# End of slots, end of output projections and operand rings in a two-layer diffusion backbone on one core

## Reference, cut to what matters

```python
def even_mixer(h_lat, h_ctx, ...):        # layer 0
    z = h_lat @ w_in
    a = spatial_gating(z[..., :1024])     # 4 groups of 128, chunks of 128 positions
    q, k, v = ...                         # 8 heads, 2 key/value heads, 128 wide, rmsnorm, rotary
    return concatenate([a, attention(q, k, v)]) @ w_out          # 1536 -> 1024 (and the context's)

def odd_mixer(h_lat, h_ctx, ...):         # layer 1
    c = silu(layernorm(dwconv31(a * sigmoid(g))))                # 512 channels
    q = rmsnorm(z_q) @ w_uq; k, v = rmsnorm(z_kv) @ w_ukv        # 8 heads, 128 + 64 rotary
    return concatenate([c, attention(q, k, v)]) @ w_out          # 1536 -> 1024

def conv_ffn(h, w_in, conv_w, conv_b, w_out):
    z = h @ w_in                                                 # 1024 -> 2 x 2816
    return (silu(dwconv3(z[..., :2816])) * z[..., 2816:]) @ w_out

# every layer
x = x + gate1 * rmsnorm(mixer(rmsnorm(x, g1) * (1 + scale1) + shift1))
x = x + gate2 * rmsnorm(conv_ffn(rmsnorm(x, g3) * (1 + scale2) + shift2))
```

## Time and profile before

| | |
|---|---|
| median of 3 runs | 1823.19 us (1819.68 to 1828.9) |
| profiled execution, its time | 1824.78 us |
| profiled execution, its span | 1823.0 us |
| TensorE busy | 1750.0 us, 96% |
| VectorE, ScalarE, GpSimd busy | 1121.0, 684.2, 182.0 us |
| mean granted clock of TensorE | 0.988 |
| HBM read | 163.31 MB, 91 GB/s |

### The profile page before, as it was taken

One profiled execution on the slowest core, in us unless ns is written; L12 is line 12 of the kernel. 1 busy time (PEld: TensorE's weight loads), 2 busy tenths in 40 slices (PEclk: granted clock), 3 DMA queues, 4 the chain that ended last, 5 costly groups with the idle time before them and its releaser, 6 DMA issues.

```text
span 1823.0 us, 23635 instructions
## 1 busy us (share of the span) xinstructions
PE 1750.0 (96%) x9274; PEld 1470.9 (81%) x9274; DVE 1121.0 (61%) x1662; ACT 684.2 (38%) x1123; POOL 182.0 (10%) x200
## 2 busy tenths in 40 slices
PE   6999999999999999999999999999989899999998
PEld 4777899777888888887777888789977788887776
DVE  4776777777676765644444578778766544444554
ACT  4343256544422121223243444354545433223342
POOL 1077400001200000000000110111210200000000
PEclk9999999999999999999999999999999899999999
DMA  9433100131234335421112122200012132222221
GB/s 363 145 118 105 46 1 1 58 104 47 104 130 148 141 136 196 172 106 70 69 50 90 47 95 71 77 17 1 2 70 71 50 111 92 92 102 105 92 94 68
DMA packets 30994, 166.77 MB, mean 91 GB/s; under 512 B 4144, under 2 KB 4656, under 8 KB 16688
## 3 DMA queue, kind: packets, MB, share of 16 engines
q1 hardware_dynamic: 29024, 163.60, 24.6%
q10 hardware_dynamic: 1872, 1.82, 0.4%
HBM read 163.31 MB, written 2.10 MB: 91 GB/s over the span
## 4 chain that ended last, share of the span: by engine, by line
PE 85%; DVE 7%; ACT 3%; issue 2%; DVEq 1%; DMA 1%; POOL 0%; ACTq 0%; SPq 0%
PE PS L292 12%; PE PS L294 12%; PE PS L296 12%; PE PS L582 8%; PE PS L584 7%; PE PS L583 7%; PE PS L1085 5%; PE PS L319 3%; PE PS L320 3%; PE PS L321 3%; PE PS L1070 2%; DVE w_lo L281 2%; DVE cat_od L2040 1%; DVE pre_tmp_pre L486 1%; ACT w_hi L275 1%
## 5 line engine op out<-in xcount | busy, mean ns | idle before, releaser
L292 PE MATMUL PS<-HT,w_hi 128*128 128x512 f32 (+1 forms) x1232 | 378.3, 355 | 10.6 <-DVE HT L492 5.0
L294 PE MATMUL PS<-HT,w_hi 128*128 128x512 f32 (+1 forms) x1232 | 370.1, 349 | 0.0
L296 PE MATMUL PS<-HT,w_lo 128*128 128x512 f32 (+1 forms) x1232 | 370.0, 349 | 0.0
L281 DVE TENSOR_TENSOR w_lo<-w_raw,w_hi 128x2048 fp32r<-128x2048 f32 x103 | 237.8, 2309 | 154.1 <-ACT w_hi L275 149.6
L582 PE MATMUL PS<-w_hi,a_ring 128*128 128x512 f32 x680 | 274.9, 404 | 13.7 <-DVE a_ring L658 5.6
L583 PE MATMUL PS<-w_lo,a_ring 128*128 128x512 f32 x680 | 266.5, 392 | 0.0
L292 PEld LDWEIGHTS PS<-HT,w_hi 128*128 128x128 f32 x1232 | 206.5, 189 | 52.0 <-issue 7.0
L275 ACT ACTIVATE w_hi<-w_raw 128x2048 fp32r<-128x2048 f32 x103 | 196.4, 1907 | 135.9 <-PEq L616 69.3
L296 PEld LDWEIGHTS PS<-HT,w_lo 128*128 128x128 f32 x1232 | 206.7, 189 | 31.0
L294 PEld LDWEIGHTS PS<-HT,w_hi 128*128 128x128 f32 x1232 | 206.9, 189 | 30.8
L957 DVE SCALAR_TENSOR_TENSOR yb<-PS,cws,yb 128x511 f32<-128x511 f32 (+1 forms) x132 | 83.2, 658 | 168.9 <-ACTq L923 164.6
(11 more groups left out here) (305 smaller groups left out, 2596.5 us busy)
## 6 DMA issues: line engine op xcount, KB each, us to landing
w_raw<-wpack SPq DMA_DIRECT2D x103, 1024.0 KB, 4.8
m_raw<-modu SPq DMA_DIRECT2D x80, 512.0 KB, 4.0
mod_raw<-modw SPq DMA_DIRECT2D x8, 1024.0 KB, 12.0
X<-x SPq DMA_DIRECT2D x1, 2048.0 KB, 8.3
out<-X SPq DMA_DIRECT2D x4, 512.0 KB, 2.6
X<-ctx SPq DMA_DIRECT2D x1, 1024.0 KB, 10.6
alnb<-aln ACTq DMA_DIRECT2D x1, 512.0 KB, 4.2
csn<-rope_ev ACTq DMA_DIRECT2D x1, 256.0 KB, 2.6
```

The costliest lines, as they stand in the source:

```text
L281: nc.vector.tensor_tensor(w_lo[r][:, :], w_raw[r][:, :], w_hi[r][:, :].bitcast(F32), ALU.subtract).then_inc(wl_ready, 1)
L292: nc.tensor.matmul(o, wh, xh, start=start, stop=False)
L294: nc.tensor.matmul(o, wh, xl, start=False, stop=False)
L296: last = nc.tensor.matmul(o, wl, xh, start=False, stop=stop)
```

## The change

Four things are done together.

1. The drains at slot ends go. `w_used` of a slot is raised by the first matmul of the next slot, `a_used` of a column half's last part by the second matmul of the next half.
2. The ends of `evo`, `ffo0` and `odo` go by pairs of token tiles: both first quads of a pair, then both second quads; transposes of tiles 0 and 1 stand ahead of the second quads of the last pair. The orders of ScalarE, VectorE and GpSimd follow. `pre3` has eight transposes ahead too, and four of its eight affines are on ScalarE, with a drain each.
3. Parts are in rings of three; the feed-forward projections' first three parts are made ahead: 0 and 1 before the last slot is evacuated, 2 within it. In `ffo0` token tile 5 of q=0 and q=1 is made after q=1. Gate rows of the feed-forward projections start at q=3, the diagonal of the first at q=0.
4. odo's first weight turn is at q=3, not q=1. The channel norm starts at unit 22; the convolution has three steps a unit up to unit 13; the reciprocal is in two halves, in units 29 and 30; `beside_out` is spread over q=0, 2, 3, 4 (norm) and q=4, 6, 7 (SiLU).

The diff, cut to its core:

```diff
-        def split_mm(outs, wh, wl, xs, start, stop):
+        def split_mm(outs, wh, wl, xs, start, stop, slot_done=False, parts_done=None):
 
             last = None
-            for o, (xh, _) in zip(outs, xs):
-                nc.tensor.matmul(o, wh, xh, start=start, stop=False)
-            for o, (_, xl) in zip(outs, xs):
-                nc.tensor.matmul(o, wh, xl, start=False, stop=False)
+            for i, (o, (xh, _)) in enumerate(zip(outs, xs)):
+                mm = nc.tensor.matmul(o, wh, xh, start=start, stop=False)
+                if slot_done and i == 0:
+                    mm.then_inc(w_used, 1)
+            for i, (o, (_, xl)) in enumerate(zip(outs, xs)):
+                mm = nc.tensor.matmul(o, wh, xl, start=False, stop=False)
+                if parts_done is not None and i == 0:
+                    mm.then_inc(parts_done, 8)
...
+        def pre_affine_high(act, st, layer, which, i0, i1):
+
+            for i in range(i0, i1):
+                act.wait_ge(S(st, "tr"), since(st, "tr") + i + 1)
+                if i >= 6:
+                    low = "lo_odd" if i % 2 else "lo_even"
+                    act.wait_ge(S(st, low), since(st, low) + (i - 6) // 2 + 1)
+                nc.scalar.activation(pre_tmps[st][i % 6][:, :], PS[:, pre_bank(st, i), 0:256], ACT.Identity,
+                                     bias=modc[:, layer, 3 * which * KD + i, 0:1], scale=prescale[:, i, 0:1])\
+                    .then_inc(S(st, "aff"), 1)
+                act.drain()
+                nc.scalar.activation(HT[:, 0, 0, i, :], pre_tmps[st][i % 6][:, :], ACT.Copy).then_inc(S(st, "hi"), 1)
...
+                        first = g == 0 and mt == 0 and k == 0
                         last = split_mm([o], w_hi[r][:, cols], w_lo[r][:, cols], [(HT[:, g, 0, k, :], HT[:, g, 1, k, :])],
-                                        k == 0, k == KD - 1)
+                                        k == 0, k == KD - 1, first, S("evo", "a_used") if first else None)
...
-        def a_high(q, kt):
-
-            return a_ring[q % 2] if q < kt else a_ring[(q - kt) % 8]
+        def first_of_ffn(st, q):
+
+            return q == 0 and st in ("ffo0", "ffo1")
+
+        def second_of_ffn(st, q):
+
+            return q == 1 and st in ("ffo0", "ffo1")
+
+        def a_high(st, q, kt):
+
+            if q >= kt:
+                return a_ring[(q - kt + 6) % 8]
+            return a_ring[6] if first_of_ffn(st, q) else (a_second if second_of_ffn(st, q) else a_ring[q % 3])
+
+        def a_low(st, q):
+
+            return a_ring[7] if first_of_ffn(st, q) else a_ring[3 + q % 3]
...
-                    if q == 2 and before is not None:
+                c = q - (2 if before is None else 3)
+                if 0 <= c < len(gate_chunks(tiles)):
...
+                held = before is not None and tiles == NT and q < 2
+                for t in range(NT - 1 if held else tiles):
                     if h == 1 and k == 0:
...
-                    last = products(q, j, h, k, n, t)
+                    last = products(q, j, h, k, n, t, q > 0 and t == 0 and (j == 0 or k == 0), h == 1 and t == 0 and k == 0)
                     if k == kt - 1:
                         last.then_inc(S(st, "acc"), 1)
-                if k == kt - 1:
-                    pe.drain().then_inc(S(st, "a_used"), 1)
-                else:
+                if held and q == 1:
+                    pe.wait_ge(S(before, "evac"), JF)
+                    for p, (_, jp, hp, kp) in enumerate(out_ktiles(kt)[0:2]):
+                        products(p, jp, hp, kp, n, NT - 1).then_inc(S(st, "a_used"), 1)
+                elif k < kt - 1 and not held:
                     last.then_inc(S(st, "a_used"), 1)
-                if j == 3:
-                    pe.drain().then_inc(w_used, 1)
...
-            four(0, 0)
-            for t in range(1, tiles):
+            for t in range(0, tiles, 2):
                 four(0, t)
-                if chunk is not None and t == 1:
+                four(0, t + 1)
+                if chunk is not None and t == 0:
                     m_sum(pe, chunk)
-                if chunk is not None and t == 2:
-                    m_turn(pe, chunk)
-                ahead = norm is not None and PRE_AHEAD[norm] and t == tiles - 2
-                if ahead:
+                if norm is not None and t == 2:
                     if chunk is not None:
                         pe.wait_ge(m_evac, chunk + 1)
                     pre_transposes(pe, norm, 0, 4)
-                four(1, t - 1)
-                if ahead:
+                four(1, t)
+                if chunk is not None and t == 0:
+                    m_turn(pe, chunk)
+                if norm is not None and t == 2:
                     pre_transposes(pe, norm, 4, KD)
-            four(1, tiles - 1)
-            pe.drain().then_inc(S(st, "a_used"), 8)
-            pe.drain().then_inc(w_used, 1)
...
-                    at_q[q] = s + 1
+                    at_q[q + 2 if st == "odo" and q == 1 else q] = s + 1
...
-                if h == 0 and q >= 2:
-                    act.wait_ge(S(st, "a_used"), since(st, "a_used") + q - 1)
-                if h == 1:
-                    act.wait_ge(S(st, "a_used"), since(st, "a_used") + kt + (k - 7 if k >= 8 else (k > 0) - 1))
+                if h == 0 and q >= 3:
+                    act.wait_ge(S(st, "a_used"), since(st, "a_used") + q - 2)
+                if h == 1 and k >= 2:
+                    act.wait_ge(S(st, "a_used"), since(st, "a_used") + kt + max(0, k - 7))
...
-                gate_row(q - 2)
+                if q == 0:
+                    gate_row(0)
+                elif q >= (3 if before is None else 4):
+                    gate_row(q - (2 if before is None else 3))
...
+                pre_high(act, sp, 0, 1)
                 round_hi(act, n_next)
+                pre_high(act, sp, 1, 4)
                 square(2)
+                pre_affine_high(act, sp, 1, 1, 4, 6)
                 square(3)
-                pre_high(act, sp, 0, 4)
+                pre_affine_high(act, sp, 1, 1, 6, KD)
...
+            gated(0)
+            update(0)
+            gated(1)
+            update(1)
+            pre_mean(dve, sp, 0)
+            pre_mean(dve, sp, 1)
+            pre_xn(dve, sp, 0)
+            pre_xn(dve, sp, 1)
...
-                pre_xn(dve, sp, 1)
+                affine(0, 4)
                 take_lo(dve, n_next)
-                affine(0, 4)
                 gated(2)
+                affine(4, 6)
                 update(2)
                 gated(3)
                 update(3)
-                affine(4, KD)
+                affine(6, KD)
                 pre_mean(dve, sp, 2)
                 pre_mean(dve, sp, 3)
+                dve.wait_ge(S(sp, "aff"), since(sp, "aff") + KD)
...
+                if last:
+                    act.wait_ge(S(st, "evac"), JF - 1)
+                    part(0)
+                    part(1)
...
+                if last:
+                    part(2)
...
+                if q == 0:
                     act.wait_ge(S("cln", "var"), 2)
                     nc.scalar.activation(nh_b[:, :], rs_b[:, :], ACT.Sqrt).then_inc(S("cln", "rstd"), 1)
-                if q == 7:
-                    for j in range(4):
+                if q in (4, 6, 7):
+                    for j in {4: (0,), 6: (1, 2), 7: (3,)}[q]:
                         act.wait_ge(S("cln", "nrm"), j + 1)
...
-                conv_steps(min(3 if 2 <= u < 10 else 2, 31 * 4 - sum(taps)))
+                conv_steps(min(3 if 2 <= u < 14 else 2, 31 * 4 - sum(taps)))
...
-                    nc.vector.reciprocal(rs_b[:, :], mu[:, :]).then_inc(S("cln", "var"), 1)
+                    nc.vector.reciprocal(rs_b[:, 0:256], mu[:, 0:256])
+                if u == CLN + 8:
+                    nc.vector.reciprocal(rs_b[:, 256:512], mu[:, 256:512]).then_inc(S("cln", "var"), 1)
...
-                if q == 4:
+                if q == 2:
                     dve.wait_ge(S("cln", "rstd"), 1)
                     nc.vector.tensor_tensor(rs_b[:, :], nh_b[:, :], nh_b[:, :], ALU.mult)
                     dve.drain()
                     nc.vector.tensor_tensor(rs_b[:, :], rs_b[:, :], mu[:, :], ALU.mult)
                     dve.drain()
-                if q == 5:
+                if q == 3:
                     nc.vector.tensor_scalar(rs_b[:, :], rs_b[:, :], -0.5, 1.5, ALU.mult, ALU.add)
                     dve.drain()
                     nc.vector.tensor_tensor(rs_b[:, :], rs_b[:, :], nh_b[:, :], ALU.mult)
                     dve.drain()
-                    for j in range(4):
+                if q in (3, 4):
+                    for j in range(2 * q - 6, 2 * q - 4):
                         nc.vector.tensor_tensor(cat_od[:, 8 + j, :], cat_od[:, 8 + j, :], rs_b[:, :], ALU.mult)\
                             .then_inc(S("cln", "nrm"), 1)
```

213 lines of the change are left out of this document (104 added, 109 removed).

## The result

The changed kernel takes 1793.49 us (median of 4, 1790.29 to 1794.47) against 1822.39 (median of 4, 1819.68 to 1828.9): a ratio of 0.9822, 95% interval 0.9801 to 0.9843, 29 us less. The profiled execution went from 1824.78 to 1792.66 us, its span from 1823.0 to 1790.7.

A forecast was written before the change was run, and what follows sets the result against it. TensorE bounds the kernel, busy 96% of the span; the change removes time in which it starts nothing or runs at half clock. Terms sum to 31.0 us off the 1823.2 median, 1792.2, stated as 1793, range 1785 to 1808.

The forecast's parts named there:

- Drains: TensorE's slot, half and stage ends: each drain costs 0.42 us between starts; removing them gives 12.5 of the sum.
- rival B: Projections: VectorE or ScalarE takes back what drains give, only the stalls pay; 1804 us, chance 0.2.
- Tile pairs: Ends of evo, ffo0 and odo: two quads ahead of the transposes, not three, add 0.75 us idle each.
- ffo0: Start at once with early parts, q=2 held by w_lo for 0.9 us; 3.3 gained, plus 3.9 from drains.
- ffo1: Earlier start, wait of 2.15 us at q=2, half-clock stretch gone if clock holds; 3.4 gained, plus 3.0 from drains.
- odo: Wait of 1.8 us at q=4, wait of 2.1 before q=7 gone; 8.4 gained by q=8.
- the sums lie two units earlier now (0.86 of matmul off the tail): Odd attention's end: layer norm's sums come two units earlier, taking 0.86 us off the tail; odo starts at 1349.6.
- pre3: After odo: losses fall from 11.5 to 6.0 us, gain 5.5, range 2 to 9; about 2.5 left at k=6.
- Clock: Five stretches around the changed code at half clock, each after a gap of 2.1 us or more between starts.
- C: The five waits that stay each bring the lower clock, 5 times 1.6 = 8 us; 1801 us, chance 0.1.
- D: Slot ends: a signal on a matmul costs TensorE as much as the drain, 12.5 stay away; 1805 us, chance 0.05.
- E: Slot boundaries: w_used one matmul late makes all 28 slots wait, slower; 1832 us at 1.4 each, chance 0.02.

The follow-up runs named there:

- run 1: The kernel before with the drains' signals moved to matmuls and nothing else; ratio 0.9924 to the kernel before, about 14 us less.
- run 2: The changed kernel with a drain, without a signal, ahead of each matmul that carries w_used; ratio 0.9895 to the kernel before.
- run 6: The changed kernel with the endings of evo and ffo0 as before, pairs only at odo; ratio 0.9845 to the kernel before.
- run 4: The changed kernel with odo's first weight turn back at q=1; ratio 0.9852 to the kernel before.
- run 5: The changed kernel with convolution pace, channel norm's first unit (24) and one-piece reciprocal as before; ratio 0.9847 to the kernel before.
- run 8: The changed kernel with pre3's low parts 6 and 7 ahead of tile 3's gate product and power; ratio 0.9838 to the kernel before.
- run 9: The changed kernel with odo's channel-norm steps moved to q=4 and 5 and first SiLU to q=5; ratio 0.9848 to the kernel before.
- run 7: The changed kernel with odo's ending and pre3 as before; ratio 0.9852 to the kernel before, median 1798.6 us.
- run 3: The changed kernel with both feed-forward projections' q=0 and q=1 parts made after the last slot's last matmul; ratio 0.9852 to the kernel before.
- run 10: The changed kernel with ffo1's second-slot weights and q=2 low part made ahead of the last feature tile's evacuation; ratio 0.9844 to the kernel before.
- run 12: The changed kernel with runs 5, 6, 11, a modified 8, and later odo norm and SiLU together; 1788.48 us, ratio 0.9796 to the kernel before.
- run 11: Run 10 with ffo1's two gate rows also moved from q=3 and 4 to q=7 and 8; ratio 0.9836 to the kernel before.

## Why the prediction was right, and where it was not

I had said 1793 for the median and 1793.8 for the profiled execution; measured were 1793.5 and 1792.7. The sum of 31.0 stands against 28.9 by medians and 32.1 by the profiled times. Part by part:

- **Drains.** I had 12.5. The trace of run 1 gives 11.7, run 2 13.3, both with some clock in them. The size of one was too low: 0.50, since the second matmul behind it is late too, which I did not read. VectorE took the difference back: two waits that grew by 0.5 and 1.1, and the new ones in ffo1 and odo. Of these the sum had only the late lower half of ffo1 and the two drains of evo that are partly covered; the rest was in rival B. That the total came out near 12.5 is two errors that cancel.
- **Tile pairs.** New idle time of 0.75 each; measured 0.89, 0.80 and 0.80 behind evo, ffo0 and odo (1.05, 0.96 and 0.96 between starts), and run 6 has evo 0.80 and ffo0 1.04 shorter without it.
- **ffo0.** Wait at q=2: predicted 0.9, measured 0.58 idle (0.75 between starts). The clock stayed whole, as in the sum. The two stages gained 7.6, the terms for them came to 6.5; the nine drains at 0.50 in place of 0.42 (0.7) are most of the rest.
- **ffo1.** Predicted a wait of 2.15 at q=2, measured 2.02 between starts. 6.8 gained, 6.4 predicted. That the clock held was luck in this execution: it halved there in runs 2, 4, 5, 8 and 9 and not in 6 and 7, behind the same wait.
- **odo.** From q=0 to q=8 predicted 25.5, measured 25.7; the wait at q=4 was put at 1.8 and is 1.9. The wait of 2.1 in the kernel before that I put at q=7 is at q=6: its matmul starts at 1377.55, two k-tiles before q=8 at 1383.55. It is gone either way.
- **A step that failed** is "the sums lie two units earlier now (0.86 of matmul off the tail)". I booked the two matmuls as gone, while they only stand earlier in the same attention, where VectorE kept them waiting 0.71. With the 0.7 for the third steps I expected that stage 1.0 shorter; it is 0.7 longer. Run 5 shows that the whole move loses 0.5.
- **pre3.** Predicted a gain of 5.5; run 7 puts the ending at 4.8. The wait at k=6 is 3.2, not 2.5: both updates took 1.7 in place of 1.29, GpSimd having begun a low part just before each (last section). I named the right wait, but not the next bound: run 8 shows that xn of tiles 2 and 3 holds TensorE as long.
- **Clock.** The sum had some 8 us of half clock coming back at the changed places, and five stretches did: at ffo0, odo, two of three in pre3, and ffo1. Three more are missing where the change took out drains alone: at the even mixer's start, in the first attention and in the odd mixer, 4.1 us without the idle time in them. The first attention has one stretch in all but one of the later traces, but the two mixers were luck in this pair of executions: where the program is the same, the even mixer has its second stretch in runs 3, 4, 7 and 10, the odd mixer in 3, 5 to 8, 10 and 12. They made up for the 1.7 lost in the attention, so the total of the profiled executions was closer than its terms. By the medians the gain is 28.9, 2.1 under the sum.

I also read the clock too simply: not every stretch stands behind a gap of 2.1 us. The one at 1432 in the kernel before stands behind two waits of 0.89, ahead of the eight transposes and behind them (TensorE's timeline and the window of the kernel before):

```profile
1431.85 0.47 PE L292 MATMUL PS<-HT,w_hi 128*128 128x256 f32 x1 [0.89 <-DVE HT L492]
...
1432.00:1435.00 3.00, 3.00 (x16) 3.00 (x16) 2.34 (x6) 0.84 (x2) 1.84 (x3) 0.50 0.69 287
```

Of the rivals, B was true at some places (odo's q=6 and pre3 in run 1, the four slot starts of ffo1 in run 1, the second halves of odo and ffo1 there and in the changed kernel), C (every wait that stays brings the lower clock) at some waits in some executions. D and E fell.

For C spoke a rule of the Trainium skill's page "TensorE: Matmul & The Clock Gate" that frequent short idle times make the clock swing. It stands in the section "A second HAM failure mode: psum-queue depth-cycling" and not in the one that I named. It is not borne out as a rule here: the traces show one stretch of 3.4 us or twice that behind a single wait (the shortest 1.81 us, in run 2) and not behind each wait as long, and one stretch, at 1432, behind two waits of 0.89.

## What to carry to other kernels

Read a drain's cost as the distance between starts over the next two instructions, not as the idle time, and move its signal onto an instruction that comes anyway. Before an order on the second engine is changed to shorten a wait, sum what that engine has to do until the instruction waited for: the four such edits here (runs 8 to 11) each moved the wait to a later step and gained nothing alone. Work that is moved earlier on the bottleneck engine is not saved.

## What the runs showed of the hardware

- A drain of TensorE costs 0.38 us, one that signals a semaphore 0.50; the same signal on a matmul costs nothing that shows (0.23 between starts). The idle time in the record, 0.26 for the one that signals, shows about half.
- The same part of a program has half-clock stretches in some executions and not in others. Behind the wait of about 3 us at the odd mixer (1175 in the changed kernel) the lower clock lasted 3.4 us in some, 6.8 in others, and did not come in one (run 9); behind the wait of 2.0 at ffo1 it came in runs 2, 4, 5, 8 and 9 and not in the changed kernel, 6 and 7. A stretch of 3.4 costs 1.7 us in a dense stream (ffo1 126.7 against 125.0), and less where TensorE then waits for another engine anyway: in pre3, 0.9 for one and 2.1 for two (248.7 and 249.9 against 247.8). This goes with the spread within one kernel: of nine executions of the kernel before beside run 12, the fastest took 1820.68 us at a mean granted clock of 0.994, the slowest 1829.02 at 0.988.
- Of a VectorE update of X (128x1024) and a GpSimd low part (128x256) that meet, the one that started first keeps its time and the other is longer. In `evo` the update started 0.15 us ahead: it took 1.28 us as alone, and the low part 1.72 in place of 0.73. In `odo` the low part started 0.26 and 0.11 ahead, and the updates took 1.75 and 1.70; the first of these low parts took 0.93, with a VectorE low part of 0.41 begun just before it. VectorE's and GpSimd's timelines of the changed kernel, in `evo` and `odo`, and the updates by stage (ns min/median/max):

```profile
442.65 1.28 DVE L848 SCALAR_TENSOR_TENSOR X<-O_both_evo,rstd,X 128x1024 f32<-128x1024 f32 x1
442.80 1.72 POOL L513 TENSOR_TENSOR HT<-pre_tmp_pre,HT 128x256 fp32r<-128x256 f32 x1 [1.40 <-ACT HT L520]
...
1411.47 0.93 POOL L513 TENSOR_TENSOR HT<-pre_tmp_pre,HT 128x256 fp32r<-128x256 f32 x1
1414.20 0.73 POOL L513 TENSOR_TENSOR HT<-pre_tmp_pre,HT 128x256 fp32r<-128x256 f32 x1
...
L848 DVE SCALAR_TENSOR_TENSOR X<-O_both_evo,rstd,X x6: 1278/1284/1286, 428.3 to 456.1; 128x1024 f32<-128x1024 f32 x6
L848 DVE SCALAR_TENSOR_TENSOR X<-O_both_odo,rstd,X x4: 1284/1490/1753, 1396.0 to 1414.3; 128x1024 f32<-128x1024 f32 x4
```
